# A hybrid decoder step on one core: the last attention unit's exponentials, turn and values moved behind the first half's gate

## The reference

```python
def swa_prompt(u, w_in, q_norm_w, k_norm_w, sinks, w_out):
    q, k, v, g = attn_project(u, w_in, q_norm_w, k_norm_w)
    ...
    o = attend_with_sink(qb, keys, vals, mask[None, :, None, None], sinks)
    ...
    out = (o * jax.nn.silu(g)) @ w_out
    return out, k[:, -WINDOW:], v[:, -WINDOW:]
```

## Time and profile before

| | |
|---|---|
| time, median of 3 runs | 960.2 us (960.0 to 960.73) |
| the profiled execution: its time, its span | 960.25 us, 958.4 us |
| PE busy in it | 937.8 us, 98% |
| DVE, ACT, POOL busy | 560.0, 477.2, 322.7 us |
| mean granted PE clock | 0.997 |

### The profile page before, as it was taken

The page is one execution under the profiler, slowest core; times in us unless marked ns, Lnnn a source line. Parts: engine busy times, 40 slices in busy tenths (PEclk is TensorE's granted clock), DMA queues, the critical chain, the costliest instruction groups (busy, mean ns, idle before and its releaser), DMA issues.

```text
span 958.4 us, 18425 instructions
## 1 busy us (share of the span) xinstructions
PE 937.8 (98%) x7252; PEld 872.2 (91%) x7252; DVE 560.0 (58%) x1428; ACT 477.2 (50%) x943; POOL 322.7 (34%) x257
## 2 busy tenths in 40 slices
PE   9999999999999999999999999999999999999898
PEld 8998899989998899988998889998899989998787
DVE  4234421444225432447688679865898568986782
ACT  6335713365235623267537565446562565626852
POOL 3442244223441243224624232622434223442500
PEclk9999999999999999999999999999999999999999
DMA  7522221342143221211433825247152572427303
GB/s 212 181 74 74 78 92 56 107 151 86 49 116 151 90 88 52 89 23 45 123 101 112 231 62 168 89 118 222 47 162 91 149 206 69 126 88 216 108 12 105
DMA packets 144614, 105.91 MB, mean 111 GB/s; under 512 B 10754, under 2 KB 135860, under 8 KB 144464
## 3 DMA queue, kind: packets, MB, share of 16 engines
q1 hardware_dynamic: 134536, 100.19, 34.6%
q10 hardware_dynamic: 9992, 4.54, 1.9%
HBM read 91.99 MB, written 16.79 MB: 113 GB/s over the span
## 4 chain that ended last, share of the span: by engine, by line
PE 87%; DVE 8%; issue 2%; DMA 1%; ACT 1%; SPq 0%; POOL 0%; DVEq 0%; ACTq 0%
PE pp L1285 22%; PE pp L1287 21%; PE pp L1286 21%; PE pS L1395 2%; PE pO L1619 2%; PE pO L1615 2%; PE pT_ L1605 2%; PE pO L1442 1%; PE pO L1441 1%; DVE s_in L2310 1%; PE pO L1566 1%; PE pS L1538 1%; DMA w_raw_buf<-in_w_attn_in 1%; DVE cv L2025 1%; PE pS L1576 1%
## 5 line engine op out<-in xcount | busy, mean ns | idle before, releaser
L706 POOL TENSOR_TENSOR w_lo_buf<-w_raw_buf,w_hi_buf 128x512 fp32r<-128x512 f32 x214 | 278.9, 1334 | 477.7 <-ACT w_hi_buf L782 305.4
L1285 PE MATMUL pp<-h_hi,w_hi_buf 128*128 128x280 f32 (+2 forms) x1248 | 378.7, 303 | 1.6 <-DVE rb L1999 1.6
L1287 PE MATMUL pp<-h_hi,w_lo_buf 128*128 128x280 f32 (+2 forms) x1248 | 363.2, 291 | 0.0
L1286 PE MATMUL pp<-h_lo,w_hi_buf 128*128 128x280 f32 (+2 forms) x1248 | 362.7, 291 | 0.0
L1285 PEld LDWEIGHTS pp<-h_hi,w_hi_buf 128*128 128x128 f32 x1248 | 235.1, 188 | 11.1 <-issue 8.1
L1286 PEld LDWEIGHTS pp<-h_lo,w_hi_buf 128*128 128x128 f32 x1248 | 235.2, 188 | 5.4 <-issue 4.8
L1287 PEld LDWEIGHTS pp<-h_hi,w_lo_buf 128*128 128x128 f32 x1248 | 235.4, 189 | 0.0
L782 ACT ACTIVATE w_hi_buf<-w_raw_buf 128x2048 fp32r<-128x2048 f32 (+1 forms) x55 | 104.1, 1892 | 47.4 <-DMA w_raw_buf<-in_w_ssm_in 29.8
L1805 DVE TENSOR_TENSOR x<-x,pp 128x272 f32<-128x272 f32 (+2 forms) x120 | 53.1, 442 | 81.9 <-PE pp L1287 81.2
L1285 PE MATMUL pp<-og_hi,w_hi_buf 128*128 128x280 f32 (+2 forms) x256 | 75.6, 295 | 3.0 <-DVE x L1805 1.9
L1287 PE MATMUL pp<-og_hi,w_lo_buf 128*128 128x280 f32 (+2 forms) x256 | 74.5, 291 | 0.0
(11 more groups left out here) (357 smaller groups left out, 1615.3 us busy)
## 6 DMA issues: line engine op xcount, KB each, us to landing
w_raw_buf<-in_w_attn_in SPq DMA_DIRECT2D x16, 1024.0 KB, 5.2
w_raw_buf<-in_w_ssm_in SPq DMA_DIRECT2D x16, 1024.0 KB, 6.3
w_raw_buf<-in_w_attn_out SPq DMA_DIRECT2D x8, 1024.0 KB, 5.3
s_in<-in_state_ssm SPq DMA_DIRECT2D x32, 256.0 KB, 3.9
out<-s_in SPq DMA_DIRECT2D x32, 256.0 KB, 3.9
w_raw_buf<-in_w_ssm_out SPq DMA_DIRECT2D x8, 1024.0 KB, 6.5
seg<-a_scratch SPq DMA_DIRECT2D x12, 512.0 KB, 5.0
w_raw_buf<-in_w_attn_in SPq DMA_DIRECT2D x8, 512.0 KB, 6.3
```

The source lines that it names most:

```text
L706: ins = pool.tensor_tensor(low_buf(n)[:, piece], raw[n % RAW_SLOTS][:, piece], high_buf(n)[:, piece].bitcast(F32), ALU.subtract)
L1285: pe.matmul(dst, hi[:, k, cols], a_hi[:, k, tk], start=(k == 0), stop=False)
L1286: pe.matmul(dst, hi[:, k, cols], a_lo[:, k, tk], start=False, stop=False)
L1287: mm = pe.matmul(dst, lo[:, k, cols], a_hi[:, k, tk], start=False, stop=(k == depth - 1))
```

## The change

It touches the end of the last group (s = 3) on three engines. On ACT, `exps(3, 5)` and `copy_pT(3, 4)` leave the unit loop; `copy_pT(3, 4)` stands behind `silu_last(0)`, and the exponentials behind `high_last(0)`, with a table load (`exp_tables`) ahead of them. On PE, `transposes(3, 5)` moves from ahead of n = 0 to behind n = 1, and `values(3, 5)` from behind n = 1 to behind n = 2. On DVE, `normalise(3, 5)` moves behind the first `add_out`, and `gate_last(1)` and `low_last(1)` each by one piece.

```diff
@@ ACT @@
                 for u in range(1, UNITS):
+                    if (s, u) == (GROUPS - 1, UNITS - 1):
+                        break
                     copy_pT(s, u - 1)
                     if u == 2:
                         copy_o(s, 0)
                     exps(s, u)
-                    if (s, u) == (GROUPS - 1, UNITS - 1):
-                        break
@@
             silu_last(0)
+            copy_pT(GROUPS - 1, UNITS - 2)
             act.wait_ge(s_done, UNITS * GROUPS)
             high_last(0)
+            exp_tables()
+            exps(GROUPS - 1, UNITS - 1)
             copy_o(GROUPS - 1, UNITS - 2)
             copy_pT(GROUPS - 1, UNITS - 1)
             silu_last(1)
@@ PE @@
                 if s + 1 < GROUPS:
                     project("kv", s + 1, 0, 0)
-                transposes(s, UNITS - 1)
-                if s + 1 < GROUPS:
+                    transposes(s, UNITS - 1)
                     project("kv", s + 1, 0, 1)
                     values(s, UNITS - 1)
             for n, (t, half) in enumerate(out_order(GROUPS - 1)):
                 project("out", GROUPS - 1, t, half)
                 if n == 1:
+                    transposes(GROUPS - 1, UNITS - 1)
+                if n == 2:
                     values(GROUPS - 1, UNITS - 1)
@@ DVE @@
                 else:
-                    normalise(s, UNITS - 1)
                     break
@@
             for n, (t, half) in enumerate(out_order(GROUPS - 1)):
-                if n == 2:
+                if n == 1:
+                    normalise(GROUPS - 1, UNITS - 1)
+                if n == 3:
                     gate_last(1)
-                if n == 3:
+                if n == 4:
                     low_last(1)
                 add_out(GROUPS - 1, t, (half,))
```

## The result

| | before | changed |
|---|---|---|
| median of 6 runs | 960.26 us (959.04 to 960.89) | 963.53 us (963.25 to 964.55) |
| ratio, 95% interval | | 1.0037 (1.0027 to 1.0047) |
| span of the profiled execution | 958.4 us | 961.4 us |
| PE, ACT busy | 937.8, 477.2 us | 938.0, 480.3 us |

The kernel is 3.3 us slower; 963.6 was forecast. ACT is busy 3.1 us longer, of which the two added table loads are 2.6.

What follows compares the result with a forecast made beforehand. PE was taken as the bound, busy 937.8 of 958.4 us. The terms -1.51, +2.0, +0.85, +2.2, -0.2 gave 3.3 us, 3.36 by the starts of n = 4: 960.25 + 3.36 = 963.6 us, with a shift range of 2.6 to 4.2 us.

Steps and rivals of the forecast that it cites:

- Half 0: First half's output pieces on PE: n = 0 starts at 431.64 instead of 433.15, 1.51 us earlier.
- The wait for the turn: PE, behind n = 1: idle from 434.76 to 436.75, 2.0 us, until DVE's normalise of the last unit is done.
- The wait for half 1: PE, behind n = 3: idle 2.2 us until n = 4, which starts at 444.6 instead of 441.24.
- The sum: Start of n = 4: -1.51, +2.0, +0.85, +2.2 and -0.2 give 3.3 us later; by the two starts 3.36.
- +0.85: PE's transposes of the last unit hold it 0.85 us, formerly between two waits, now counted in full.
- Nothing behind n = 4 gives it back: From n = 4 to the end: all later work is tied to this chain, so the 3.36 us shift stays.
- Loads are hidden: Rival on ACT: the two added loads cost nothing, n = 4 is 1.6 us later, 961.9 us; chance 0.12.
- A switch costs more than its load: Rival on ACT: each added table switch costs 1.3 us more, n = 4 at 447.2, 966.2 us; chance 0.04.
- The clock falls: Rival on PE: after two 2 us waits the clock falls, two pieces' 3.2 us double, 966.8 us; chance 0.06.

Runs made afterwards that it cites:

- the filled one: Changed kernel plus three useless matmuls on PE ahead of the last unit's transposes and three behind n = 3; 964.5 us (1.0034), measured again 963.79 us (1.0037).
- the later turn: Changed kernel with PE's transposes(3, 5) moved behind n = 2 and values(3, 5) behind n = 3; 964.2 us, ratio 1.0043.
- SiLU in the gaps: Kernel before with first-half SiLU and both its table loads behind unit 4's exponentials, normalise(3, 5), turn, values and second SiLU also reordered; 960.48 us, 0.9998.
- the third load in ACT's wait: Changed kernel with two of the second half's four SiLU, and the third table load, ahead of ACT's copy of the turned weights; 963.18 us, ratio 1.0030.

## Why the prediction was right

- **Half 0.** Forecast 1.51 us earlier, measured 1.51. `copy_pT(3, 4)` ended 0.6 us or more ahead of the values that read it, as worked out, so nothing was late there.
- **The wait for the turn.** Forecast 2.0 us, measured 1.69, a difference of 0.31. The turn came 7.30 us behind the gate piece instead of 7.46, mainly because ACT's rounding ended 0.46 us behind the product's end (430.71 against 430.25) and not 0.63. The other 0.15 is in the counting: I let the wait begin with the slot behind the last matmul of n = 1, and the profile counts PE as busy until that matmul's end, 434.00.
- **The wait for half 1.** Forecast 2.2 us, measured 2.03; n = 4 forecast 3.36 us late, measured 3.2 in all five profiles of this order (the changed kernel three times, the filled one twice). That ACT's path beats PE's by 0.45 us there was shown by taking it off: +2.75 instead of +3.2.
- **The sum.** Its three positive terms (+2.0, +0.85, +2.2) are not independent costs, as the later turn shows: take one wait away and the next grows. The sum held because it was checked against the two starts of n = 4. Counted by causes: turn and values later +2.85, half 0 earlier -1.47, the two added loads +1.83.
- **Nothing behind n = 4 gives it back.** The shift at `sum_x` is that at n = 4 within 0.2 us when the clock holds. From there to the end the profiles scatter: +3.90 us at the end in the first profile of the changed kernel, +4.26 in the third. The spans differ by less, 3.0 and 3.7 us, since the gate piece came 0.9 and 0.6 us earlier than in the profile before. That 963.53 lies within 0.1 us of 963.6 is in part luck: the interval on the ratio stands for 2.6 to 4.5 us more than before, and the two later measurements of the changed kernel give 2.6 and 3.0 us.
- **The rivals.** "Loads are hidden" is out: without them the kernel is 1.8 us faster in the shift and about 2 in the whole time. "A switch costs more than its load" is out: 430.73 + 1.28 = 432.01, and the exponentials start at 432.02 in the changed kernel. "The clock falls" came about in two of three profiles, which I had given 0.06, but with a price of 0.45 us at `sum_x` where I had put 3.2: I had taken two whole pieces at half clock, and it was thirteen of 24 matmuls, with a wait of 0.57 us at n = 8 under them and 0.3 us more at n = 12 and n = 14, where PE without the fall comes close behind DVE's additions. With the turn one piece later the clock fell too (+3.20 at n = 4, +3.62 at `sum_x`).
- **A version that beats both** was not found. The best, with SiLU in the gaps, equals the kernel before.

## What to carry to other kernels

When work is moved ahead of a late step, follow the late step to its own reader first: here the early half gained 1.5 us and the late half, which had no slack, lost 3.2. A step may be started early for nothing if it goes into its engine's gaps; put in front of a step on the chain, it can cost its length, and here a table load in each direction. And price a removed or added instruction by what stands right behind it on the chain: a load of 1.28 us was worth 0.28 us in one order, and in the other two loads were worth 1.8 of their 2.6 us.

## What the hardware showed that I had not expected

PE's granted clock fell to 0.50 for about 3.3 us, starting 1.5 us behind the end of a wait of 2.0 us, though PE was busy without a break when it fell. In another execution of the same kernel, with a wait of 2.00 us at the same place, it stayed at 1.00. With a wait of 3.52 us at n = 4 (the later turn) it fell, with waits of 1.6 us and less at n = 4 it did not. A wait of 2.19 us ahead of n = 0 was followed by a fall, one of 0.77 us there was not. In these two other kernels the windows put the fall earlier, some 0.2 us (2.19) and 0.3 us (3.52) behind the end of the wait.

The scatter of the whole time has a place. In the next layer DVE computes `y_lo` while POOL computes the low parts of the weights. In the changed kernel the four pieces of DVE took 2.85 us, in the kernel with SiLU in the gaps 4.51 us, and there PE waited 0.9 us for them and 0.5 us for an addition. DVE's group in the changed kernel:

```profile
605.56 2.85 DVE L2194 TENSOR_TENSOR y_lo<-z,y_hi 128x384 fp32r<-128x384 f32 x4
```

DVE's in the kernel with SiLU in the gaps:

```profile
601.85 4.51 DVE L2193 TENSOR_TENSOR y_lo<-z,y_hi 128x384 fp32r<-128x384 f32 x4
...
607.51 2.75 DVE L2193 TENSOR_TENSOR y_lo<-z,y_hi 128x160 fp32r<-128x160 f32 x2
```

POOL's beside it, in the same kernel:

```profile
604.67 5.41 POOL L706 TENSOR_TENSOR w_lo_buf<-w_raw_buf,w_hi_buf 128x512 fp32r<-128x512 f32 x4 [0.76 <-PE pp L1289]
```

Over all profiles single instructions of DVE range there from 0.55 to 1.72 us at 128x384 and from 0.31 to 1.42 us at 128x160, long where POOL's lie beside them. Three of the profiles (the first filled one, the third load in ACT's wait, SiLU in the gaps) have both of these waits, and their shift grows by 1.4 to 1.8 us at this place; the others have at most 0.24 us of wait there. Whether the meeting of the two engines lengthens DVE's instructions was not tested by itself. The growth is larger than several of the effects above, and a reason to compare such kernels at a mark close to the edit as well as by their whole times.
